# Ending a two-block fp32 kernel in token rows, with padded attention keys and modulation tiles placed elsewhere

## What is computed

```python
def sandwich(x, fn, pre_g, post_g, shift, scale, gate, res_w):
    hn = rmsnorm(x, pre_g) * (1 + scale[:, None, :]) + shift[:, None, :]
    y = rmsnorm(fn(hn), post_g)
    return x + res_w * gate[:, None, :] * y
...
mod = (jax.nn.silu(c) @ w_mod[i] + b_mod[i]).reshape(B, N_SUB, 3, D_MODEL)
```

## Time and profile before

| what | value |
|---|---|
| median of 3 runs | 4138.98 us (4126.71 to 4141.5) |
| profiled execution, its own time | 4134.65 us |
| profiled execution, span of the trace | 4132.9 us |
| mean granted clock of TensorE | 0.961 |
| busy: PE, DVE, ACT, POOL | 3892.6, 2340.6, 1289.0, 815.4 us |

### The profile page before, as it was taken

One profiled execution on the slowest core, in us unless ns is written; L12 is line 12 of the kernel. 1 busy time (PEld: TensorE's weight loads), 2 busy tenths in 40 slices (PEclk: granted clock), 3 DMA queues, 4 the chain that ended last, 5 costly groups with the idle time before them and its releaser, 6 DMA issues.

```text
span 4132.9 us, 48106 instructions
## 1 busy us (share of the span) xinstructions
PE 3892.6 (94%) x19280; PEld 3138.3 (76%) x19280; DVE 2340.6 (57%) x3011; ACT 1289.0 (31%) x1685; POOL 815.4 (20%) x580
## 2 busy tenths in 40 slices
PE   7997999999799999999888999999999999989998
PEld 5666788866678878887667888788877878777886
DVE  3778655477865555557557434633554544555334
ACT  3443222335332232222543222222233333222222
POOL 2112444311245536653212000000000000000000
PEclk8999999999899999999998999999999999998999
DMA  4112444421234435553212333233212122112331
GB/s 135 60 41 68 125 142 138 123 62 52 62 107 146 145 107 159 147 148 80 63 47 65 103 92 102 74 100 102 92 59 79 57 67 71 57 53 70 102 94 60
DMA packets 556441, 377.72 MB, mean 91 GB/s; under 512 B 30121, under 2 KB 553866, under 8 KB 556218
## 3 DMA queue, kind: packets, MB, share of 16 engines
q1 hardware_dynamic: 555642, 372.55, 30.7%
q10 hardware_dynamic: 576, 2.10, 0.1%
HBM read 372.44 MB, written 2.17 MB: 91 GB/s over the span
## 4 chain that ended last, share of the span: by engine, by line
PE 81%; DVE 14%; ACT 2%; issue 2%; SPq 0%; DMA 0%; DVEq 0%; ACTq 0%
PE bank L437 59%; PE bank L473 4%; PE bank L445 3%; PE bank L803 2%; DVE w_lo L415 2%; PE bank L818 2%; PE bank L1979 1%; PE bank L2004 1%; PE bank L811 1%; PE bank L2025 1%; DVE hgrn_scores L1288 1%; DVE norm_tmp L1504 1%; DVE k_decayed L1302 1%; ACT w_hi L406 1%; DVE squares_sum L624 1%
## 5 line engine op out<-in xcount | busy, mean ns | idle before, releaser
L437 PE MATMUL bank<-H_hi,w_hi 128*128 128x512 f32 x2384 | 979.3, 411 | 1.0 <-DVE w_lo L415 0.9
L437 PE MATMUL bank<-H_hi,w_lo 128*128 128x512 f32 x2384 | 935.2, 392 | 0.0
L437 PE MATMUL bank<-H_lo,w_hi 128*128 128x512 f32 x2384 | 933.5, 392 | 0.0
L415 DVE TENSOR_TENSOR w_lo<-w_raw,w_hi 128x2048 fp32r<-128x2048 f32 (+3 forms) x285 | 727.9, 2554 | 275.5 <-ACT w_hi L406 264.7
L406 ACT ACTIVATE w_hi<-w_raw 128x2048 fp32r<-128x2048 f32 (+3 forms) x285 | 529.1, 1857 | 302.0 <-DMA w_raw<-in_ffn_w_up 131.7
L437 PE MATMUL bank<-U_hi,w_hi 128*128 128x512 f32 x1408 | 557.6, 396 | 20.4 <-DVE U_lo L1168 14.5
L437 PEld LDWEIGHTS bank<-H_hi,w_hi 128*128 128x128 f32 x2384 | 449.3, 188 | 152.3 <-issue 68.2
L437 PE MATMUL bank<-U_hi,w_lo 128*128 128x512 f32 x1408 | 551.4, 392 | 0.0
L437 PE MATMUL bank<-U_lo,w_hi 128*128 128x512 f32 x1408 | 550.9, 391 | 0.0
L437 PEld LDWEIGHTS bank<-H_hi,w_lo 128*128 128x128 f32 x2384 | 449.1, 188 | 98.0 <-issue 0.5
L437 PEld LDWEIGHTS bank<-H_lo,w_hi 128*128 128x128 f32 x2384 | 450.2, 189 | 87.3 <-issue 6.7
(11 more groups left out here) (337 smaller groups left out, 4946.9 us busy)
## 6 DMA issues: line engine op xcount, KB each, us to landing
w_mod_raw<-in_w_mod SPq DMA_DIRECT2D x144, 512.0 KB, 6.2
w_raw<-in_ffn_w_gate SPq DMA_DIRECT2D x88, 512.0 KB, 4.0
w_raw<-in_ffn_w_up SPq DMA_DIRECT2D x88, 512.0 KB, 5.3
w_raw<-in_dil_w_in SPq DMA_DIRECT2D x36, 1024.0 KB, 5.1
w_raw<-in_w_mlp_in SPq DMA_DIRECT2D x32, 1024.0 KB, 5.5
w_raw<-in_w_mlp_out SPq DMA_DIRECT2D x32, 1024.0 KB, 5.2
w_raw<-in_ffn_w_down SPq DMA_DIRECT2D x32, 1024.0 KB, 5.0
w_raw<-in_w_in SPq DMA_DIRECT2D x16, 1024.0 KB, 5.2
```

The lines of the kernel that those rows point to most:

```text
L415: dve.eng.tensor_tensor(WL[u % SLOTS][:, 0:n], RAW[u % SLOTS][:, 0:n], WH[u % SLOTS][:, 0:n].bitcast(F32), ALU.subtract).then_inc(lo_done. ...
L437: mm = pe.eng.matmul(bank[0:m, :], w[:, k, c0:c0 + m], r[:, k, :], start=(k == 0 and i == 0), stop=(k == kt - 1 and i == 2))
```

## The change

Three parts, which have nothing to do with each other in the code.

**The end.** The last product has procedures of its own. While it runs, TensorE transposes each tile of X (`turn_x`, bank 6) and each finished tile of Y (`turn_y`, bank 7, multiplied by its column of gate * post_g first, on DVE) between the matmuls, and ACT copies the banks into `XROW` and `YROW`, which hold tokens on partitions. Then the factor 1/rms is one number per partition, so that the spread isn't needed, and four DVE operations of 128x1024 make the output rows. SP stores each of them. The meeting of the engines and the epilogue are gone.

**Padded keys.** `KPAD[0]` and `KPAD[1]` hold the first key head on partitions 0 to 63 and 64 to 127, zeros on the other half; later the unused halves of `Z[:, ZK]` and `KSW` are cleared for the second key head. `scores` multiplies all 128 rows of `Z[:, h // 2]`, where the zeros mask the other head's queries. For each layer that adds two copies on ACT and four memsets on DVE, all of 64x512, and three waits on TensorE.

**Modulation tiles.** A tile is no longer loaded with unit u when unit u - 2 or u - 3 is one of 14 units called crowded: `mix` and `mixh` (10 to 14 and 57 to 61), the last `down` unit of each layer of the first stack (46, 93), and units 127 and 142, the last before two borders of the second stack. That leaves out 20 places up to unit 165, so that the last tile goes with unit 165 and not with 145. The tile's product still comes two units later.

```diff
-        MOD_LAG, MOD_BEHIND = 4, 2
-        MOD_TILES = min(72 * DEPTH, len(units) - MOD_LAG)
+        MOD_LAG = 2
+        MOD_TILES = 72 * DEPTH
+        crowded = {u for l in range(DEPTH) for stage in (("mix", l), ("mixh", l)) for u in lin[stage]}
+        crowded |= {lin[("down", l, 3)][-1] for l in range(DEPTH)} | {lin[("ffn_down", 0, 0, 2)][-1], lin[("mla_out",)][-1]}
+        mod_unit = [u for u in range(2, len(units)) if not {u - 3, u - 2} & crowded][:MOD_TILES]
+        mod_at = {u: m for m, u in enumerate(mod_unit)}
...
-        for m in range(MOD_TILES):
-            mod_after.setdefault(MOD_LAG + m, []).append(m)
+        for m, u in enumerate(mod_unit):
+            mod_after.setdefault(u + MOD_LAG, []).append(m)
...
-            return min(MOD_TILES, max(0, u - MOD_LAG))
+            return sum(v + MOD_LAG < u for v in mod_unit)
...
+        KPAD = [at(f"k_padded{i}", u_at + 4 * K + 2 * K * i, [P, L]) for i in range(2)]
+        k_zero, k_padded, k_blank = line("k_padding_cleared"), line("k_padded_ready"), line("k_halves_cleared")
...
+            put(24, ("kpad", 0))
...
                 if (kind, i) == ("scores", 0):
                     pe.eng.wait_ge(qk_done.sem, 6 * (l + 1))
+                    pe.eng.wait_ge(k_zero.sem, l + 1)
+                    pe.eng.wait_ge(k_padded.sem, 2 * (l + 1))
+                if (kind, i) == ("scores", len(items) // 2):
+                    pe.eng.wait_ge(k_blank.sem, l + 1)
...
+            elif kind == "kpad":
+                act.eng.wait_ge(qk_done.sem, 6 * l + 2)
+                for half, src in enumerate((Z[:, ZK, :], KSW)):
+                    rows = slice(HEAD * half, HEAD * half + HEAD)
+                    ae.activation(KPAD[half][rows, :], src[rows, :], ACT.Copy).then_inc(k_padded.sem, k_padded.add())
+                    act.eng.wait_ge(k_padded.sem, k_padded.made)
...
+            elif kind == "vturn":
+                dve.eng.wait_ge(k_padded.sem, 2 * (l + 1))
+                ve.memset(Z[0:HEAD, ZK, :], 0.0).then_inc(dve.step.sem, dve.step.add())
+                dve.eng.wait_ge(dve.step.sem, dve.step.made)
+                ve.memset(KSW[HEAD:P, :], 0.0).then_inc(k_blank.sem, k_blank.add())
+                dve.eng.wait_ge(k_blank.sem, k_blank.made)
...
+            dve.eng.memset(KPAD[0][HEAD:P, :], 0.0).then_inc(dve.step.sem, dve.step.add())
+            dve.eng.wait_ge(dve.step.sem, dve.step.made)
+            dve.eng.memset(KPAD[1][0:HEAD, :], 0.0).then_inc(k_zero.sem, k_zero.add())
+            dve.eng.wait_ge(k_zero.sem, k_zero.made)
...
-                keys = Z[:, ZK, :] if kv == h % 2 else KSW[:]
+                keys = (KPAD[h % 2][:], Z[:, ZK, :] if h % 2 else KSW[:])[kv]
...
-                        "segs": [(Z[r:r + HEAD, h // 2, b * P:(b + 1) * P], keys[r:r + HEAD, :], 0, None)], "n": L, "scale": HEAD ** -0.5,
+                        "segs": [(Z[:, h // 2, b * P:(b + 1) * P], keys, 0, None)], "n": L, "scale": HEAD ** -0.5,
...
+        XROW, YROW = at("x_rows_out", h_at, [P, NB, D]), at("y_rows", h_at + 16 * K, [P, NB, D])
+        x_turned, x_rows, y_gated, y_turned, y_rows, out_rows, out_stored = (line(n) for n in (
...
+        def turn_x(pe, t):
+            pe.eng.wait_ge(x_rows.sem, t)
+            for b in range(NB):
+                mm = pe.eng.transpose(banks[6][:, b * P:(b + 1) * P], X[:, t, b * P:(b + 1) * P], EYE)
+            mm.then_inc(x_turned.sem, x_turned.add())
+
+        def turn_y(pe, t):
+            pe.eng.wait_ge(y_gated.sem, t + 1)
+            pe.eng.wait_ge(y_rows.sem, t)
+            for b in range(NB):
+                mm = pe.eng.transpose(banks[7][:, b * P:(b + 1) * P], XY[t % 2][:, b * P:(b + 1) * P], EYE)
+            mm.then_inc(y_turned.sem, y_turned.add())
+
+        def last_down_pe(pe):
+            at_point = {}
+            for t in range(DT):
+                at_point[8 * t + 2] = (turn_x, t)
+                at_point[8 * t + 13] = (turn_y, t)
+            points = iter(range(8 * DT))
+
+            def weave():
+                turn, t = at_point.get(next(points), (None, 0))
+                if turn:
+                    turn(pe, t)
+            for u in lin[("ffn_down", 1, 1, 2)]:
+                pe_unit(pe, u, weave)
+            pe_running_sums(pe)
+            turn_y(pe, DT - 1)
+
+        def row_copy(act, turned, bank, dst, ready, t):
+            act.eng.wait_ge(turned.sem, t + 1)
+            act.eng.activation(dst[:, :, t * P:(t + 1) * P], bank[:].rearrange("p (b c) -> p b c", c=P), ACT.Copy).then_inc(ready.sem, ready.add())
+            act.eng.wait_ge(ready.sem, ready.made)
+
+        def last_down_act(act):
+            stage = ("ffn_down", 1, 1, 2)
+            for u in lin[stage]:
+                if u != lin[stage][-1]:
+                    split_hi(act, u + AHEAD)
+                for j in range(2):
+                    t = 2 * (u - lin[stage][0]) + j
+                    if t == 0:
+                        act.eng.activation(NOTE[:, 1:2], NOTE[:, 1:2], ACT.Sqrt).then_inc(act.step.sem, act.step.add())
+                        act.eng.wait_ge(act.step.sem, act.step.made)
+                    row_copy(act, x_turned, banks[6], XROW, x_rows, t)
+                    if t:
+                        row_copy(act, y_turned, banks[7], YROW, y_rows, t - 1)
+                    place, turn = acc_place[units[u]["tiles_at"] + j]
+                    act.eng.wait_ge(acc_free[place].sem, turn)
+                    if t >= 2:
+                        act.eng.wait_ge(sq_summed.sem, sq_summed.next(act, 0 if t == 3 else 1))
+                    act.eng.activation(SQ[t % 2][:], Y[:, t, :], ACT.Square).then_inc(sq_run.sem, sq_run.add())
+                    act.eng.wait_ge(sq_run.sem, sq_run.made)
             act_std(act, D, True)
-
-        def sandwich_post_dve(dve):
-            dve_rstd(dve)
-            for t in range(DT):
-                last = t == DT - 1
-                signal = rbc_used if last else dve.step
-                dve.eng.scalar_tensor_tensor(NT[2][:], Y[:, t, :], AFF[:, 1, 1, t:t + 1], banks[5][:], ALU.mult, ALU.mult).then_inc(signal.sem, signal.add())
-                dve.eng.wait_ge(signal.sem, signal.made)
-                dve.eng.tensor_tensor(X[:, t, :], X[:, t, :], NT[2][:], ALU.add).then_inc(dve.step.sem, dve.step.add())
-                dve.eng.wait_ge(dve.step.sem, dve.step.made)
+            row_copy(act, y_turned, banks[7], YROW, y_rows, DT - 1)
+
+        def last_down_dve(dve):
+            stage, ve = ("ffn_down", 1, 1, 2), dve.eng
+            for u in lin[stage]:
+                if u != lin[stage][-1]:
+                    split_lo(dve, u + AHEAD)
+                for j in range(2):
+                    t = 2 * (u - lin[stage][0]) + j
+                    if t >= 2:
+                        add_squares(dve, t - 1)
+                    bank, free = acc_take(dve, u, j)
+                    ve.tensor_tensor(Y[:, t, :], Y[:, t, :], bank[:], ALU.add).then_inc(free.sem, free.add())
+                    dve.eng.wait_ge(free.sem, free.made)
+                    if t >= 2:
+                        dve.eng.wait_ge(y_turned.sem, t - 1)
+                    ve.tensor_scalar(XY[t % 2][:], Y[:, t, :], AFF[:, 1, 1, t:t + 1], None, ALU.mult).then_inc(y_gated.sem, y_gated.add())
+                    dve.eng.wait_ge(y_gated.sem, y_gated.made)
+            dve.eng.wait_ge(std_ready.sem, std_ready.next(dve))
+            ve.reciprocal(RSTD[:, 0:NB], STD[:, 0:NB]).then_inc(dve.step.sem, dve.step.add())
+            dve.eng.wait_ge(dve.step.sem, dve.step.made)
+            dve.eng.wait_ge(x_rows.sem, DT)
+            dve.eng.wait_ge(y_rows.sem, DT)
+            for b in range(NB):
+                ve.scalar_tensor_tensor(XROW[:, b, :], YROW[:, b, :], RSTD[:, b:b + 1], XROW[:, b, :], ALU.mult, ALU.add).then_inc(out_rows.sem, out_rows.add())
+                dve.eng.wait_ge(out_rows.sem, out_rows.made)
+
+        def store_rows(sp):
+            for b in range(NB):
+                sp.eng.wait_ge(out_rows.sem, b + 1)
+                sp.eng.dma_start(io["out"][0, b * P:(b + 1) * P, :], XROW[:, b, :]).then_inc(out_stored.sem, out_stored.add(16))
+            sp.eng.wait_ge(out_stored.sem, out_stored.made)
...
+                if (i, s, part) == (1, 1, 2):
+                    last_down_pe(pe)
+                else:
+                    pe_linear(pe, ("ffn_down", i, s, part))
...
-            norm_pe(pe, running=True)
...
-            sandwich_post_act(act)
...
-            sandwich_post_dve(dve)
...
-                if 0 <= u - MOD_BEHIND < MOD_TILES:
-                    sp_mod(sp, u - MOD_BEHIND)
+                if u in mod_at:
+                    sp_mod(sp, mod_at[u])
...
+            store_rows(sp)
...
-            sync_all(pe, "pe")
-            epilogue_pe(pe)
...
-            sync_all(act, "act")
-            epilogue_act(act)
```

30 lines of the change are left out of this document (7 added, 23 removed).

## The result

The changed kernel takes 4071.1 us (median of 4 runs, 4066.0 to 4072.5) against 4140.2 for the kernel before on the same chip (4 runs, 4126.7 to 4142.5). The ratio is 0.9837, with a 95% interval of 0.9815 to 0.986. The profiled execution took 4066.01 us, where the one of before took 4134.65: 68.6 us less, and the forecast had 51.3. (4066.01 is the fastest of the four; the other three took 4070.8 to 4072.5.)

The account below looks back on a forecast made before the run. TensorE was taken to bound the kernel (81% of the last chain), with VectorE holding the chain in stretches such as the recurrences. 17.5 + 19 + 5 + 9.8 = 51.3 us off 4134.65 gave 4083 us, range 4067 to 4106.

Parts of the forecast that it names:

- Padded keys, 17.5: Mixers of both layers: full-height score products shorten TensorE's stream by 0.36 us each; 17.5 us kept, bounds 8 and 24.
- to keep three quarters: Mixers: VectorE, next to be late, leaves three quarters of the score products' saving, 17.5 us for both layers.
- VectorE bounds the mixers: Rival, chance 0.15: VectorE's full middle and fixed order limit the mixers; padding gives 5 us, kernel 4096.
- a TensorE that waits for VectorE in the mixers: Mixers: a sign that would show the forecast wrong; no size was given.
- Height doesn't matter: Rival, chance 0.06: the score products' 1.24 us has another cause; padding in the mixers gives 0, kernel 4101.
- Tiles away from the recurrence, 19: Recurrences of both layers: without GpSimd's modulation tiles, VectorE's SBUF operations aren't lengthened; 19 us, bounds 12 and 21.
- Borders, 5: Stage borders: moved modulation tiles stop lengthening VectorE operations; 9 us less 4 for restarts, net 5, bounds 0 and 9.
- Together 9 us come off: Borders behind the mixers and in the second stack: summed VectorE lengthening removed, 9 us before deducting restarts.
- The end, 9.8: Last projection 6.6 us longer from transposes, tail behind it 16.4 us shorter; net 9.8 us, bounds -2 and 11.
- the rival of the falling clock: Rival, chance 0.03: in the last projection the granted clock falls to 1.2 GHz, doubling its 44 us; kernel 4127.
- SP's queue: Rival, chance 0.02: tiles waiting on SP delay weights by one unit at six restarts, 66 us lost; kernel 4149.
- all of it is had: Rival, chance 0.07: whole kernel gains every part in full, 24 + 21 + 9 + 10 = 64 us, giving 4071.

Follow-up runs that it names:

- padding alone: The kernel before with only the padded keys of the change added: 4110.8 us, ratio 0.9938.
- the end alone: The kernel before with only the new procedures for the last product and output added: 4127.6 us, ratio 0.9976.
- VectorE's work taken out: The changed kernel with 12 of the 31 convolution taps of each channel tile left out: 4070.5 us, ratio 0.9836.
- tiles alone: The kernel before with only the modulation tiles' new places added: 4093.9 us, ratio 0.9895.
- GpSimd's work put back: The changed kernel with four lots of GpSimd work added per recurrence: 4069.7 us started beside score rounds, 4088.2 us started beside SBUF-only products.

## Why the prediction was right, and where its sum was short

The sum was 51.3 against 68.6 us in the profiled executions. By its own steps:

- **Padded keys, 17.5.** The mechanism held: 0.39 us for a product between projection matmuls, where I took 0.36. With padding alone the mixers gave 20.1 us, but that the number is near is partly luck, since some of it is the clock, which the forecast had left out. The clean comparison is the kernel with the tiles moved against the changed kernel: the mixers' mean clock is 0.98 and 1.00 in the one, 0.99 and 1.00 in the other, and the new end doesn't touch them (176.1 and 181.0 us with the end alone). There padding takes 10.4 and 9.9 us off TensorE's busy time, 3.7 and 3.2 come back as waits, and each mixer is 6.7 us shorter: 13 us for 17.5. I had put 11.5 a mixer for the price, and to keep three quarters; it was 10, and two thirds. The price was too high because only 44 of the 64 products stand between two projection matmuls: the 22 of a mixer save 8.6 of its 10 us, and the other 10 little.
- **Padded keys, the rivals.** The 18.5 us of VectorE's work taken out brought 2.3 us of the waits back, so that the rival "VectorE bounds the mixers" is wrong as a bound. Its sign, a TensorE that waits for VectorE in the mixers, is there (2.4 and 1.5 us in mixer 0), but both waits stand in the kernel before, too, at the same length; most of what came is for ACT's probabilities. "Height doesn't matter" fell with the product's price. The Trainium skill's rule that a product of few rows takes the time of 128 ("TensorE: Matmul & The Clock Gate", "Why this matters for your kernels") prices a low product between projection matmuls wrongly: 1.25 and 0.86. It fits the products inside a group, since four cost no more extra than one. Its other rule, that a change of tiling mode drains the engine ("TensorEngine Tiling (Array Packing)", "Key Properties"), agrees with that: 0.39 us for each group and not for each product.
- **Tiles away from the recurrence, 19.** 19.4 measured with tiles alone. The mechanism held: against the shortest of their kind, the lengthened VectorE operations of a recurrence add up to 10.0 and 10.2 us in the kernel before (forecast 10.7) and to nothing in the changed one; with GpSimd's work put back they are 0.6 beside the score rounds and 9.4 beside the products. Beside the padding the recurrences gave 10.5 and 12.6; padding alone shortened them by 0.9 and 2.9, and how isn't settled.
- **Borders, 5.** This is the step that failed. "Together 9 us come off" took the length by which VectorE's operations were stretched for the price of the place. At the two borders behind the mixers, where it had 4.4, the stages from the recurrence's root to the next gave 1.2 together (26.3 to 26.9 and 26.4 to 24.6). At the others three things were missing. TensorE's wait at a border stands behind a chain of such operations, so it fell by 3.3 and 4.4 us at the two borders of the second stack. The clock goes down behind a wait: 1.2 GHz for 8 us and more at one border, and for 17 us in mixer 1, where the forecast had no term at all. And every tile's product is TensorE's too: 18 of them came into feed-forward (0,1), which got 5.8 us longer, 0.32 each; the multilayer perceptrons, which lost 5 each, got 1.1 and 1.3 shorter. All stages but mixers, recurrences and end gave 13 us net, and the mixers gave 9 beside the padding's 13, nearly 8 of them in mixer 1.
- **The end, 9.8.** 6.8 us more in the last stage (forecast 6.6), 17.0 less behind it (16.4): 10.2. The clock stayed at 1.00 with 15 groups of transposes in 44 us, so the rival of the falling clock was wrong there. SP's queue blocked nothing: the modulation tiles' stretch in feed-forward (0,1) has TensorE busy 377.6 of 381.4 us.

The rival nearest to the time was "all of it is had" (4071), but for another reason: the padding gave 4 us less than forecast, the recurrences 4 more, and the clock and the borders' waits came on top. So the time was inside the range although one term was too large and the clock stood in none.

## What to carry to other kernels

Price a wait of TensorE by what the clock does behind it: look for a granted clock of 0.50 in the windows behind each wait of about 3 us. Removing such a wait can give back more than its length; here a wait that fell by 2.4 us gave 9.1, and one of 3.3 gave 5.6. For the same reason compare a part's gain only between stages whose granted clock is the same. Where products of half height stand in a stream of full-height ones, zeros up to full height pay some 0.4 us for each group, as long as the padding's own operations don't stand ahead of what TensorE waits for next. For work on GpSimd beside VectorE ask when it starts, and not how much it is.

## What the runs showed of the hardware that was not expected

- A wait of the same length, 3.3 to 3.4 us, at the same place brought the clock to 0.50 for 17 us (before, end), for 7 us (padding), or not at all (tiles, after), in kernels that differ only elsewhere.
- 17.7 us of TensorE's work at the lower clock in mixer 1 cost 7.4 us against the same work at the higher one.
- Four lots of GpSimd's work (16 us) in a recurrence cost 0.4 to 1.0 us when they lay beside operations that read PSUM, and 9 to 10 us beside products in SBUF.
- The price of low products doesn't depend on which rows they use (1.25 us in either half), nor grow with their number in a group (0.39 us for one, 0.39 or 0.40 for two, 0.39 for four).
